# Finishing work of HGRN2's last heads in other places, experts' rows turned by VectorE, and a down product begun before the last pair

## The reference

```python
def hgrn2_mixer(h, w_in, lb, norm_w, w_out):
    ...
    o = hgrn2_chunkwise(split_heads(q, HG_HEADS), split_heads(k, HG_HEADS),
                        split_heads(log_f, HG_HEADS), split_heads(i, HG_HEADS))
    o = merge_heads(head_rmsnorm(o, norm_w)).astype(h.dtype) * jax.nn.silu(g)
    return o @ w_out

def moe_swiglu(h, router_w, wg, wu, wd):
    ...
    top_logits, top_idx = lax.top_k(logits, TOP_K)
    ...
    for e in range(N_EXPERTS):
        y = y + gates[:, e:e + 1] * swiglu(t, wg[e], wu[e], wd[e])
```

## Time and profile before

| | |
|---|---|
| median of 3 runs | 1933.41 us |
| the profiled execution, its own time | 1928.41 us |
| its span in the profile | 1926.7 us |
| TensorE matmul busy | 1888.7 us, 98% of the span |
| TensorE weight load busy | 1624.8 us |
| VectorE, ScalarE, GpSimd busy | 924.8, 578.5, 723.9 us |
| mean granted TensorE clock | 0.997 |

### The profile page before, as it was taken

How to read it: one execution, slowest core, us unless ns; L and a number is a source line. 1 busy time by engine, 2 the same in 40 slices (tenths; PEclk the granted TensorE clock), 3 DMA queues, 4 the chain that set the end, 5 groups by cost and what they waited for, 6 DMA issues and landing times. The chain is left out here.

```text
span 1926.7 us, 36862 instructions
## 1 busy us (share of the span) xinstructions
PE 1888.7 (98%) x15078; PEld 1624.8 (84%) x15078; DVE 924.8 (48%) x1225; ACT 578.5 (30%) x1234; POOL 723.9 (38%) x624
## 2 busy tenths in 40 slices
PE   9999999999999999999999999999999999999997
PEld 8778744888887888888877888778999999999996
DVE  3898687667565455444436788865200000000023
ACT  1443213555533111110036657533120211111102
POOL 5755523565544334344526777652200000000011
PEclk9999999999999999999999999999999999999999
DMA  9213750222215666631211111102957578778893
GB/s 336 88 56 143 263 210 34 78 93 88 83 44 202 212 204 213 218 121 61 104 66 67 68 58 69 65 13 83 325 203 251 196 233 275 253 265 333 335 351 152
DMA packets 82824, 313.58 MB, mean 163 GB/s; under 512 B 10121, under 2 KB 10641, under 8 KB 82529
## 3 DMA queue, kind: packets, MB, share of 16 engines
q1 hardware_dynamic: 75952, 289.73, 42.5%
q0 software_dynamic: 4464, 14.35, 2.2%
q10 hardware_dynamic: 2241, 7.14, 1.0%
HBM read 301.43 MB, written 9.75 MB: 162 GB/s over the span
## 5 line engine op out<-in xcount | busy, mean ns | idle before, releaser
L261 PE MATMUL banks<-sb_act,sb_ring 128*64 128x112 f32 (+9 forms) x5088 | 621.0, 300 | 1.1 <-ACT sb_ring L468 0.7
L261 PEld LDWEIGHTS banks<-sb_act,sb_ring 128*128 128x128 f32 (+1 forms) x5088 | 592.5, 174 | 23.1 <-issue 4.5
L261 PE MATMUL banks<-sb_x_norm,sb_ring 128*128 128x256 f32 (+3 forms) x1616 | 330.9, 403 | 3.4 <-ACT sb_ring L468 2.3
L261 PEld LDWEIGHTS banks<-sb_x_norm,sb_ring 128*128 128x128 f32 (+1 forms) x1616 | 242.3, 171 | 66.5 <-issue 29.3
L3732 DVE TENSOR_TENSOR sb_act<-sb_work,banks 128x192 f32<-128x192 f32 (+7 forms) x88 | 27.2, 309 | 482.8 <-PE banks L261 475.2
L443 POOL TENSOR_TENSOR sb_ring<-sb_ring 128x512 f32<-128x512 f32 x146 | 205.1, 1405 | 102.0 <-PE banks L261 53.9
L261 PE MATMUL banks<-sb_work,sb_ring 128*64 128x256 f32 (+2 forms) x1124 | 231.6, 407 | 3.9 <-ACT sb_ring L468 2.7
L261 PEld LDWEIGHTS banks<-sb_work,sb_ring 128*128 128x128 f32 (+1 forms) x1124 | 155.9, 165 | 57.7 <-issue 35.3
L3263 POOL DMA_INDIRECT sb_work<-first_expert_rows,sb_table x8 | 7.5, 939 | 442.6 <-DMA first_expert_rows<-sb_x_norm 440.4
L3534 ACT ACTIVATE sb_work<-banks 128x192 f32<-128x192 f32 (+7 forms) x88 | 25.8, 294 | 295.2 <-PE banks L261 293.2
L2370 ACT ACTIVATE sb_work<-banks 128x256 f32<-128x256 f32 x84 | 32.3, 384 | 216.8 <-PE banks L261 216.8
(11 more groups left out here) (530 smaller groups left out, 2588.8 us busy)
## 6 DMA issues: line engine op xcount, KB each, us to landing
sb_ring<-in_w_moe_up SPq DMA_DIRECT2D x176, 512.0 KB, 4.9
sb_ring<-in_w_moe_down SPq DMA_DIRECT2D x64, 704.0 KB, 6.4
sb_act<-in_cond_w SPq DMA_DIRECT2D x84, 512.0 KB, 3.7
sb_ring<-in_w_ffn_up SPq DMA_DIRECT2D x44, 512.0 KB, 5.2
sb_ring<-in_w_h_in SPq DMA_DIRECT2D x32, 512.0 KB, 4.2
sb_ring<-in_w_in SPq DMA_DIRECT2D x28, 512.0 KB, 5.9
sb_ring<-in_w_m_in SPq DMA_DIRECT2D x24, 512.0 KB, 3.9
sb_ring<-in_w_ffn_down SPq DMA_DIRECT2D x16, 704.0 KB, 5.4
```

The source lines that it names most:

```text
L261: last = m.nc.tensor.matmul(out[part], weights[:, part], act, start=start, stop=stop, skip_group_check=skip)
```

## The change

Two parts. (A) In `stage_h` the finishing of heads 4 and 5 moves to head 7, levels 1 and 3, both halves together; head 5's root has a tile of its own; TensorE's wait at level 4 of head 7 is for heads 0 to 3 only; head 6's output is formed at level 2 of head 7; `sum_first` moves from level 3 to level 5. (B) In `stage_moe` the rows of a tile are gathered in quarters such that VectorE's block transposes turn them; ScalarE scales and shifts them in place; the rows are stored from a reordered copy made by GpSimd; the results of a rank are turned back at the next rank's first down block; and that block's first ten matmuls wait only for the first ten pairs. The diff, cut:

```diff
-        self.table = sb("table", [P, 3 * ST + GATHERS + 1 + EXPERTS + 4 * ST], U32)
+        self.table = sb("table", [P, 3 * ST + 1 + EXPERTS + 4 * ST], U32)
+        self.row_parts = sb("row_parts", [P, 4 * GATHERS], U32)
...
-        self.d_rows = dram("normed_rows", (S, D))
+        self.d_rows = dram("normed_rows", (4 * S, DG))
@@ stage_h
-    norms = [Norm(m, A[:, h:h + 1, :], m.ones128[:], H[:, 6:7, :], H[:, 7, :], m.c("eps6"), False, bank=5)
-             for h in range(HEADS)]
+    norms = [Norm(m, A[:, h:h + 1, :], m.ones128[:], H[:, 6:7, :], W[:, 0, :] if h == HEADS - 3 else H[:, 7, :],
+                  m.c("eps6"), False, bank=5) for h in range(HEADS)]
@@ tensor
-                        pe.wait_ge(head_out, 2 * EARLY)
+                        pe.wait_ge(head_out, 2 * HK)
...
-                    if h and j == VALUES:
+                    if h and j == (VALUES - 1 if h == HEADS - 1 else VALUES):
                         values(h - 1)
@@ vector
-                finishes = 1 if h == HEADS - 1 else 5
                 for j in range(1, LEVELS):
                     if j > 1:
                         if j != 4 or h in (0, HEADS - 1):
                             times(h, j)
+                        if h == HEADS - 1 and j == 5:
+                            dve.wait_ge(m.blocks_done, pairs.blocks_no(pairs.n - 1))
+                            quads.sum_first(dve)
                         take(h, j - 1)
                         add(h, j - 1)
...
-                    if h > 1 and finishes <= j <= finishes + 1:
-                        finish(h - 2, j - finishes)
-                    if h == HEADS - 1 and j == 3:
-                        dve.wait_ge(m.blocks_done, pairs.blocks_no(pairs.n - 1))
-                        quads.sum_first(dve)
+                    if 1 < h < HEADS - 2 and j in (5, 6):
+                        finish(h - 2, j - 5)
+                    if h == HEADS - 1 and j in (1, 3):
+                        for half in range(2):
+                            finish(HEADS - 4 if j == 1 else HEADS - 3, half)
@@ stage_moe
+    tokens = m.d_tokens.rearrange("(p g q) o -> p q (g o)", g=4 * GATHERS, q=QUARTER)
+    by_quarter = lambda t: t.rearrange("p (q k c) -> p k q c", q=4, c=QUARTER)
+    stored_rows = m.d_rows.rearrange("(t q) c -> t (q c)", q=4)
@@ gpsimd
+            pool.wait_ge(m.evac, done + 2)
+            for t in range(ST):
+                pool.wait_ge(row_out, t + 1)
+                give(pool, nc.gpsimd.tensor_copy(by_quarter(quartered[t]), x_rows[:, t, :].rearrange(
+                    "p (k q c) -> p k q c", q=4, c=QUARTER)), row_parted, t + 1)
+            pool.wait_ge(m.loaded[SLOTS - 1], 16 * (uses[SLOTS - 1] + 1))
+            for t in range(ST):
+                pool.dma_start(stored_rows[rows(t, P), :], quartered[t]).then_inc(row_stored, 16)
             pool.wait_ge(scattered, 16 * 2 * ST)
             pool.wait_ge(row_stored, 16 * ST)
...
-                pool.dma_start(token_rows, tokens[p], allow_slow_non_contiguous=True).then_inc(idx_in, 16)
-                pool.wait_ge(idx_in, p * 16 + 16)
+                for q in range(4):
+                    pool.dma_start(m.row_parts[rows(q, QUARTER), :], tokens[p],
+                                   allow_slow_non_contiguous=True).then_inc(idx_in, 16)
+                pool.wait_ge(idx_in, p * 64 + 64)
                 pool.sem_inc(order, 1)
+                for q in range(1, 4):
+                    part = m.row_parts[rows(q, QUARTER), :]
+                    m.glink.on(pool)(nc.gpsimd.tensor_scalar(part, part, q, None, ALU.add))
                 for i in range(first_pass(p), GATHERS):
...
+                    for q in range(4):
+                        c = 4 * i + q
+                        nc.gpsimd.indirect_dma_start(
+                            got[i % BUFS][:, rows(q, DG)], None, m.d_rows,
+                            bass.IndirectOffsetOnAxis(ap=m.row_parts[:, c:c + 1], axis=0)
+                        ).then_inc(got_sem[i % BUFS], 16)
@@ tensor
-                        if b == 4 and 0 < r <= turned_ranks:
-                            turn_result(r - 1)
...
                         if b == up:
+                            if 1 < r <= turned_ranks + 1:
+                                pe.wait_ge(y_copied, p * copies + copies_until(r - 2))
+                                pe.sem_inc(order, 1)
                             if 0 < r <= turned_ranks:
-                                pe.wait_ge(y_copied, p * copies + copies_until(r - 1))
-                                pe.sem_inc(order, 1)
-                            for i in tiles_beside(p, r):
-                                turn(i)
-                            pe.wait_ge(m.evac, p * per_pass + (base + up))
+                                turn_result(r - 1)
+                            pe.wait_ge(m.evac, p * per_pass + (base + up - 2))
...
+                            if b == up and k == KE - 1:
+                                pe.wait_ge(m.evac, p * per_pass + (base + up))
+                                pe.sem_inc(order, 1)
@@ scalar
-                act.dma_start(m.d_rows[rows(t, P), :], x_rows[:, t, :]).then_inc(row_stored, 16)
...
                     for k in range(KD):
-                        last = nc.scalar.activation(xT[:, k, rows(i, P)], ps[:, pair + k // 4, rows(k % 4, P)],
-                                                    ACT.Identity, bias=norm.shift(k), scale=norm.scale(k))
+                        x = xT[:, k, rows(i, P)]
+                        last = nc.scalar.activation(x, x, ACT.Identity, bias=norm.shift(k), scale=norm.scale(k))
...
-                        if j == 2 and 0 < r <= turned_ranks:
-                            take_result(r - 1)
...
+                    if 0 < r <= turned_ranks:
+                        take_result(r - 1)
                     for i in tiles_beside(p, r):
                         take_turned(i)
+                    if first_pass(p) and r == 0:
+                        act.wait_ge(row_stored, 16 * ST)
@@ vector
+            def turn(p, i):
+                dve.wait_ge(got_sem[i % BUFS], p * (64 * got_used[i % BUFS]) + 64 * (
+                    i // BUFS + (i % BUFS > 0) + (not first_pass(p))))
+                for q in range(4):
+                    at = i * P + q * QUARTER
+                    last = nc.vector.transpose(xT[:, :, at:at + QUARTER], got[i % BUFS][:, rows(q, DG)])
+                last.then_inc(turned, 1)
...
+                    for i in tiles_beside(p, r):
+                        turn(p, i)
```

More of the change, by code:

```diff
@@ L3342, in body @@
             def body(p):
-                def turn(i):
-                    pe.wait_ge(got_sem[i % BUFS], p * (16 * got_used[i % BUFS]) + 16 * (
-                        i // BUFS + (i % BUFS > 0) + (not first_pass(p))))
-                    if not first_pass(p) or i >= 3:
-                        pe.wait_ge(turned_out, p * GATHERS + (i - 2))
-                    for k in range(KD):
-                        last = nc.tensor.transpose(ps[:, 4 + 2 * (i % 2) + k // 4, rows(k % 4, P)],
-                                                   got[i % BUFS][:, rows(k, P)], m.c("ident"))
-                    last.then_inc(turned, 1)
                 def turn_result(r):
                     pe.wait_ge(m.evac, p * per_pass + (r * total + done + total))
-                    pe.wait_ge(turned_out, p * GATHERS + (need[min(r + 1, EXPERTS - 1)] - 1))
                     for k in range(KD):
@@ L3367, in body @@
                     pe.sem_inc(order, 1)
-                    for i in range(need[0]):
-                        turn(i)
                 for r in range(EXPERTS):
@@ L3685, in mix @@
                 for i in (2 * t, 2 * t + 1):
-                    dve.wait_ge(got_sem[i], 16 * ((1 if turn == 1 else PASSES) * got_used[i] - (i == 0) + turn))
+                    dve.wait_ge(got_sem[i], 64 * ((1 if turn == 1 else PASSES) * got_used[i] - (i == 0)) + 16 * turn)
                 a1, a2 = got[2 * t], got[2 * t + 1]
@@ L3723, in late @@
                 again.scale_tiles(m, dve)
+            def turn(p, i):
[5 more added lines that the diff above has]
+                last.then_inc(turned, 1)
             def body(p):
+                if not first_pass(p):
+                    for i in range(need[0]):
+                        turn(p, i)
                 for r in range(EXPERTS):
```

14 lines of the change are left out of this document (4 added, 10 removed).

## The result

The kernel after takes 1953.04 us (median of 4 runs, 1952.0 to 1953.58) against 1933.38 us (median of 4) for the kernel before on the same chip: a ratio of 1.010, 95% interval 1.0088 to 1.0112. It is 20 us slower, where 13.5 us less were forecast. Its profiled execution took 1953.58 us, with a span of 1951.7.

What follows compares the result with a forecast made beforehand. TensorE was taken as the bound, with matmuls busy 98% of the span. Gains of 5.0 us in heads 6 and 7 and 8.5 in the experts made 13.5, from 1933.41 to 1919.9 us, range 1916.5 to 1926.0.

Steps and rivals of the forecast that it cites:

- The gathers of tiles 1 and 2: First expert: GpSimd's copy, store, list and gather chain finishes with 6 us to spare before down block 4; cost nothing.
- slower-than-before rival: First expert: GpSimd's chain late, ScalarE in rank 0 waits for tile 2; stall of 29 us, 1949; chance 0.05.
- Turning on VectorE: First expert: VectorE's block transposition of 256 columns takes 0.5 us, 2 us for a tile, at most 5.6.
- Part B's gain: Experts' up and down blocks: 72 transposes off TensorE (8.2 us) and a removed 0.29 us wait; sum 8.5 us.
- Part A: Heads 6 and 7: reordered finishing of heads cuts TensorE's idle time and low clock; 5.0 us, ends 2 and 8.5.
- no low clock would be left there: Sign of being right: no stretch of low clock on TensorE before the end of the program.
- The waits of 1.37 and 1.78 us: Heads 6 and 7: these two TensorE waits go nearly whole, as queries come 2.4 and 4.8 us sooner.
- wait over 2.5 us at level 5 of head 7: Sign of being wrong: such a TensorE wait, instead of the forecast 1.5 us, could bring the low clock back.
- the 1.7 us put down for the clock: Head 7, 1264.40 to 1268.00: the low clock behind the 2.91 us wait goes with it, gaining 1.7 us.
- Part A gives little: Head 7: VectorE stays the bound and the wait moves from level 3 to 5; gain 0 to 2.5; chance 0.15.
- Small pieces lose against weights: First expert: 1 KB gathers land in 21 us, stalling TensorE by 5 us (3 to 8); 1924.9; chance 0.10.
- Given back in the weight stream: Experts, ranks 5 to 7: short of bytes, 2 to 4 us return as waits for blocks; 1922.9; chance 0.07.

Runs made afterwards that it cites:

- paced: Kernel after, with GpSimd waiting for the landing of the previous tile's gathers before issuing a tile's four in the first expert: 1922.97 us.
- gap: Kernel after with a GpSimd fill of 256 columns ahead of each gather, one gather every 1.56 us: 1919.97 us, one run.
- a_only: Kernel before with only the stage_h hunks of the change, nothing in stage_moe: 1931.59 us, ratio 0.9993.
- best: Kernel after with at most four gathers in flight at both trains, and the second half of head 5's finish at level 5 of head 7: 1916.32 us.
- split: Kernel before, transposes kept, with each tile's rows fetched as four gathers of 1 KB pieces: 1965.14 us.
- by32: Kernel before with each tile fetched by four gathers of 32 whole rows, 4 KB pieces: 1964.12 us.
- spaced: Kernel after with a GpSimd fill of 1024 columns ahead of each gather and no wait for landings: 1919.68 us.
- probe: Kernel after with 200 independent small fills on VectorE and 60 one-column copies on ScalarE beside the train of gathers: 1956.06 us, one run.
- late: Kernel after with eight GpSimd fills of 1024 columns between the additions and the first gather: 1957.19 us, one run.

## Why the prediction was wrong

**The step that failed** is in part B, "The gathers of tiles 1 and 2": "Tiles 1 and 2 are 8 gathers of 1.26 us ... Cost nothing". It priced the first eight of a train of 32 by when their data would be there, and for that it was close. It did not price what the train does to the other engines. The trace before has only eight gathers at a stretch in this place, too few to show it. The price, 512.69 - 482.48 = 30.2 us, stands in no term, bound or rival. Each operation that the trace didn't show was bounded from both sides; the count of 32 in a row was not looked at.

**The chain itself, term by term.** The copies took 1.04 us each, not 1.4, an issue 0.55 us for a store and 0.86 for a list load, not 1.3. The stores landed at about 1379.8, 14.5 us after the last issue, not at 1376. The list was in at 1389.5 instead of 1387, the first gather came at 1390.9 instead of 1388.5; 0.8 us of each is that the whole stage stands that much later in this execution. The slower-than-before rival named this chain but another place, ScalarE waiting for tile 2; with no slow stretch (`paced`) it never did, even with the gathers spread up to 1468. That this rival's 1949 lies near the result is chance: its stall was put on late data, and the data was not late.

**Turning on VectorE** cost less than taken, in the kernel after:

```profile
1437.05 2.72 DVE L3739 STREAM_TRANSPOSE sb_act<-sb_work 128x256 f32<-128x256 f32 x8
```

2.72 / 8 = 0.34 us for 256 columns, against 0.5 taken. The estimate of 2.5 us for a tile that was worked out from the Trainium skill (VectorE: DVE Perf Modes, The three transpose paths) was too high: four of these, 1.36 us, turn a tile.

**Part B's gain was right:** 8.5 us forecast, 491.33 - 482.48 = 8.85 measured, the same in `gap` (1832.61 - 1350.18 = 482.43).

**Part A** gave 1.8 us by the medians of `a_only` and 2.6 us by the traces, not 5.0. The two profiled executions have to be laid over each other first. The block ahead of level 5 of head 6, before and after:

```profile
1237.51 7.09 PE L261 MATMUL banks<-sb_x_norm,sb_ring 128*64 128x512 f32 x32
```
```profile
1239.95 7.09 PE L262 MATMUL banks<-sb_x_norm,sb_ring 128*64 128x512 f32 x32
```

The kernel after is 2.44 us late there, from a low clock at about 306 us that the change doesn't touch (0.76 over 302 to 316, against 1.00 in the profiled execution of before). Behind head 7, at 1286.79 against 1286.95, it is 0.16 us early: part A won 2.60. By the first landmark it is late again by 0.8, for at 1330 to 1334 the granted clock is 0.57 where it was 1.00; the prediction had said that no low clock would be left there. TensorE's timeline of the kernel after, against the earlier trace rows:

```profile
1253.42 0.69 PE L262 MATMUL banks<-sb_act 128*64 128x64 f32 x16 [1.94 <-POOL sb_act L2957]
...
1272.61 1.12 PE L262 MATMUL banks<-sb_act 128*64 128x64 f32 x16 [2.87 <-issue]
```

The waits of 1.37 and 1.78 us went, and two stayed. The first was worked out well: level 1 begins at 1253.42 - 2.44 = 1250.98, where 1251.0 was forecast, behind a wait of 1.94 us instead of 1.7. The second is the "wait over 2.5 us at level 5 of head 7" that the prediction named as its own sign of failure: 2.87 us instead of 1.5. TensorE was ready on time (about 1267.3 on the axis of before, 1267.2 forecast). VectorE was 0.9 us late: it began level 5's query at 1272.08 - 2.44 = 1269.64, not 1268.7, since head 4's finish took 5.2 us, not 4.8, and the four cross products 3.7 instead of 2.8. The rest is the query's own 0.42 us and the way to TensorE, which the sum had left out. Behind this wait the granted clock is again at 0.5, the lower level (1.2 GHz), 0.57 over 1272 to 1276, so the 1.7 us put down for the clock didn't come either. In the terms of the prediction: 6.84 - 1.94 - 2.87 + 0 = 2.0 us of idle time, not 6.84 - 1.7 - 1.5 + 1.7 = 5.3.

With half of the finish moved on (`best`), TensorE is idle for 0.27 of the 25 us shown above, and the clock is whole. The wait before level 1 stays there, 1.96 us. The rival "Part A gives little" (0 to 2.5 us) was thus right for this half, for the reason it gave.

**The other rivals.** "Small pieces lose against weights" put the landing of a gather of 1 KB pieces at 21 us; in `paced` they land in 3.5 to 7, beside the same weights. And `split` and `by32`, with 1 KB and 4 KB pieces, take 1965.14 and 1964.12 us. The rule taken there from the Trainium skill, DMA: Bandwidth & Descriptors, Queues, rings and completion order, is neither shown nor contradicted by these runs, since none shows what makes up a packet. "Given back in the weight stream" fell too: the 482.4 us between the landmarks hold all of part B's gain.

**The median.** `paced`, the change plus one wait, comes to 1922.97 us, 10.4 less than the kernel before: part B's 8.85 and about 2 of part A. That `spaced` (1919.68) and `gap` (1919.97, one run) meet the forecast of 1919.9 is partly luck. In the profiled execution of `gap` the same part A wins 4.1 us over the stretch where it wins 2.6 in the kernel after: TensorE waits there for 1.95, 0.34 and 0.46 us, in `paced` for 1.94 and 2.88, with no difference in `stage_h`. Why such executions differ wasn't tried. So the working failed in one thing that it had costed at nothing, and overrated part A besides.

## What to carry to other kernels

Splitting one indirect gather into four is no small matter even where bandwidth is free: count how many GpSimd will issue in a row. Up to eight in a row, 1.25 us apart, did about 3 us of harm at most here; in twelve or more TensorE, VectorE and ScalarE slow down, TensorE from 11 to 17 us into the train to about 5 us behind its last issue. A fill of 256 columns between two gathers (0.3 us, on an engine with time to spare) or a wait for the tile before removes it whole here. When an engine stands idle for "issue" while no other engine or queue is loaded, look at what is issuing steadily on another engine, not for a missing operand.

## What the runs showed of the hardware

- A train of indirect gathers on GpSimd, 32 or more at one in 1.17 to 1.36 us, brings TensorE, VectorE and ScalarE down to one instruction per 0.70 us or a multiple, on a grid that they share (all three seen in `probe`). It does so with 131 KB a gather and with 512 bytes, with 1 KB and with 4 KB pieces, with the DMA engines at 0.02. At 1.56 us it doesn't. Why, the runs don't show.
- The Trainium skill, Runtime: NRT & Kernel Launch, Instruction fetch mechanics, says that each engine's sequencer fetches its next 16 KB of instructions over a DMA queue of its own while it executes the present ones, and that this is mostly hidden. The kernel before agrees: 45 instruction packets come in between 1348 and 1841 us, and TensorE shows no wait there. Whether fetching has a part in the slow stretch no run shows. In the kernel after no instruction packet lands between 1404 and 1435; in `late` one of 0.02 MB lands between 1420 and 1425, and the stretch goes on to 1444.9, but which engine it was for isn't shown. That the supply of instructions is what is held up is my reading of `probe`; retiring them slowly would look alike. This was not tried further.
- The eight whole-row gathers near the end have a milder case, 3 to 4 us long, from 8 us behind their first gather. It is there in the profiled `a_only` and not in the profiled kernel before, which have the same gathers; fills or waits remove it. Together with the low clock at about 306 us (3.4 to 6.8 us long in most of the other profiles) it would account for the 5.0 us by which that execution was quicker than its median. That is read from the profiles, not tried.
- VectorE turns 128x256 f32 in 32x32 blocks in 0.34 us; GpSimd copies 128x1024 f32 in 1.04 us (both in the kernel after).
